# mLSTM heads run between the blocks of their own input projection, one core of a Trainium2 chip

## The chip, the cores and the metric

The kernel runs on one core of one Trainium2 chip. The metric is the device time of one execution in microseconds, before and after the change. Engines are named as in the profile: PE (TensorE), DVE (VectorE), ACT (ScalarE), POOL (GpSimd), SP (SyncE, which issues the weight transfers).

## What is computed

Two two-layer transformer blocks one after the other on 256 tokens of width 1024, in float32, with a squared-ReLU MLP after every mixer. The change touches the last mixer alone, an mLSTM:

```python
proj = h @ w_in                       # 1024 columns q,k; 1024 v; 1024 output gate; 8 gate columns
qk = silu(causal_depthwise_conv(qk, conv_w, conv_b))      # width 4
log_f = log_sigmoid(gates_f + b_f); i_pre = gates_i + b_i
ht = mlstm_chunkwise(q, k, v, i_pre, log_f)               # 4 heads, q and k 128 wide, v 256
out = sigmoid(o_pre) * rmsnorm(ht, head_norm_w)
return out @ w_out
```

## The kernel before

Activations lie transposed: 128 features on the partitions, 256 tokens along the free dimension. A weight matrix of 1024 rows is read as *blocks* of 128 columns, two per transfer (`load`, 1 MB). Each block is split into two float32r parts: ACT writes the high part (`split_hi`, line 465) and DVE the low part (`split_lo`, line 869). The parts lie in a ring of four (`RING`), so block b + 4 is split once PE has used block b (semaphore `w_used`). For one block of the input projection `linear` has PE do 8 x 3 matmuls of 256 columns (`product`, lines 1515 to 1517) into one of PSUM banks 0 to 3, which DVE reads out (line 843 writes `mz`) with the norm's factor `rstd`. The output projections use 8 pairs of matmuls per block (`paired`, lines 1521 and 1522).

All orders are written out by hand: each engine has its own program, runs it in order, and waits on semaphores. In the input projection a loop over j, here called a *slot*, runs on each engine. In slot j PE does block j; DVE reads block j and splits block j + 4; ACT splits block j + 4. The other work of the mixer hangs on slots:

- Blocks 0 to 7 are q and k, 8 to 15 the output gate, 16 the two gate rows (`M_GATE`), 17 to 24 v.
- `CONV_AT` says after which slot a q or k block gets its convolution: even ones on DVE (lines 1306 and 846), odd ones on POOL (lines 1486 to 1494). Then SiLU: ACT runs three functions (`log_sum`, lines 752 to 756), DVE a subtraction, ACT an exponential (line 769), POOL a product (line 1498).
- The output gate goes through `log_sum`, a subtraction on DVE and an exponential on ACT (`gate_exp`, line 760).
- The gate rows: DVE reads them and adds the biases in slot 16, ACT runs two functions in slot 17 (lines 782 and 784), DVE does two scans and some row operations in slot 18 (up to line 1329, semaphore `mg_rows`), and PE transposes the result after slot 22.

After all 25 blocks the four heads run in a loop of their own. PE transposes v to tokens (`m_value_tiles`, line 1908). Per head, `m_scores` spreads two gate rows over the partitions (line 1935) and forms the scores (line 1941). DVE adds and caps the arguments (`m_args`, line 1349), ACT takes exponentials, POOL masks, DVE multiplies (`m_products`). `m_sums` forms the denominators (line 1952) and the outputs (line 1957). Then ACT and DVE alternate: absolute value (line 802), logarithm, maximum, exponential, product `m_h` and square. PE sums the squares (line 1971), ACT takes two functions, DVE scales by the norm and the output gate, ACT copies the high part of `y`, DVE subtracts for the low part (line 1378, `y_ready`). Each role has two PSUM banks, so heads overlap in pairs.

The output projection (`out_proj`) then has on DVE, per block: a reduction of the two halves of the bank (line 882), the addition to the residual `h`, the low part of a later weight block, and the low part of the normed input `x` for the next MLP (`low_part`, line 846). The first block of that MLP takes the eight pieces of `x` in order.

## Time and profile before

| | us |
|---|---|
| median of three timed runs | 1318.15 |
| lowest, highest | 1315.78, 1324.64 |
| the profiled execution | 1322.65 |
| its span, first to last instruction | 1320.7 |

The span counts from the first to the last instruction and is 1.95 us shorter than the execution's time. Times in rows are from the span's start. The mLSTM mixer lies between about 985 and 1128 us.

### The profile page before, as it was taken

How to read it: one execution, taken by the hardware profiler on the slowest of the kernel's cores; microseconds unless marked ns; L12 is line 12 of the kernel's file. 1: busy time of each engine (PE TensorE's matmuls, PEld its weight loads, DVE VectorE, ACT ScalarE, POOL GpSimd, SP SyncE). 2: the span in 40 equal slices, each digit the busy share in tenths (PEclk: the TensorE clock that was granted, in tenths of full speed). 3: DMA queues.
4: the chain of work that ended last, by engine and by line, in shares of the span. 5: the costliest groups of instructions: out<-in, count | busy, mean ns of one | idle time of the engine just before them, and what ended most of it. 6: DMA issues, size and time to landing. Idle time of an engine off the chain costs nothing.

```text
span 1320.7 us, 24258 instructions
## 1 busy us (share of the span) xinstructions
PE 1253.3 (95%) x8344; PEld 1136.4 (86%) x8344; DVE 914.6 (69%) x1553; ACT 708.5 (54%) x1257; POOL 259.2 (20%) x277
## 2 busy tenths in 40 slices
PE   7999989999999999999999889999999888999996
PEld 6998889999999888888899668888889866888885
DVE  5778865555557987865666778786558857878563
ACT  4656645654444556654454665664445745666441
POOL 4000012210001034410000003441016511344010
PEclk9999999999999999999999889999999997999998
DMA  7414235655556556555555215555554432665540
GB/s 220 139 41 148 65 96 160 191 177 176 189 159 193 190 161 190 191 191 189 192 185 180 85 33 183 185 188 182 188 181 138 160 96 64 191 187 187 183 143 32
DMA packets 202389, 205.69 MB, mean 156 GB/s; under 512 B 6080, under 2 KB 199734, under 8 KB 202314
## 3 DMA queue, kind: packets, MB, share of 16 engines
q1 hardware_dynamic: 200053, 203.12, 48.1%
q10 hardware_dynamic: 2260, 1.58, 0.4%
q8 instruction: 45, 0.74, 0.2%
q14 instruction: 31, 0.25, 0.1%
HBM read 203.61 MB, written 1.06 MB: 155 GB/s over the span
## 4 chain that ended last, share of the span: by engine, by line
PE 77%; DVE 13%; ACT 5%; issue 3%; POOL 1%; DMA 0%; DVEq 0%; SPq 0%; POOLq 0%; ACTq 0%
PE PS L1521 28%; PE PS L1522 14%; PE PS L1515 10%; PE PS L1516 9%; PE PS L1517 9%; DVE wlo L869 4%; DVE x L846 2%; ACT whi L465 1%; DVE tmp L882 1%; DVE h L892 1%; PE PS L1671 1%; PE PS L1736 1%; PE PS L1714 1%; POOL mt L1491 1%; POOL mqk L1494 1%
## 5 line engine op out<-in xcount | busy, mean ns | idle before, releaser
L869 DVE TENSOR_TENSOR wlo<-raw,whi 128x1024 fp32r<-128x1024 f32 (+1 forms) x388 | 470.5, 1214 | 217.1 <-ACT whi L465 215.3
L465 ACT ACTIVATE whi<-raw 128x1024 fp32r<-128x1024 f32 (+1 forms) x388 | 404.6, 1046 | 333.3 <-PE PS L1522 215.9
L1521 PE MATMUL PS<-x,whi 128*128 128x512 f32 x832 | 293.7, 397 | 4.8 <-DVE x L846 4.5
L1515 PE MATMUL PS<-x,whi 128*128 128x256 f32 (+2 forms) x928 | 269.8, 291 | 10.8 <-DVE x L846 5.8
L1516 PE MATMUL PS<-x,whi 128*128 128x256 f32 (+2 forms) x928 | 267.5, 288 | 0.0
L1521 PE MATMUL PS<-hid,whi 128*128 128x512 f32 x768 | 267.0, 394 | 0.0
L1517 PE MATMUL PS<-x,wlo 128*128 128x256 f32 (+2 forms) x928 | 265.2, 286 | 0.0
L1522 PE MATMUL PS<-x,wlo 128*128 128x256 f32 x832 | 235.1, 283 | 0.0
L1522 PE MATMUL PS<-hid,wlo 128*128 128x256 f32 x768 | 212.7, 277 | 0.0
L1422 POOL TENSOR_TENSOR acc<-acc,sq 128x256 f32<-128x256 f32 (+2 forms) x72 | 63.9, 888 | 717.8 <-ACT sq L493 716.7
L1521 PEld LDWEIGHTS PS<-x,whi 128*128 128x128 f32 x832 | 157.0, 189 | 42.4 <-DVE x L846 6.4
L1515 PEld LDWEIGHTS PS<-x,whi 128*128 128x128 f32 x928 | 178.7, 193 | 13.8 <-DVE x L846 7.5
L1442 POOL TENSOR_TENSOR act_s<-act_r 128x256 f32<-128x256 f32 (+1 forms) x128 | 137.6, 1075 | 226.4 <-ACT act_r L510 152.9
L1517 PEld LDWEIGHTS PS<-x,wlo 128*128 128x128 f32 x928 | 177.7, 191 | 0.0
L1516 PEld LDWEIGHTS PS<-x,whi 128*128 128x128 f32 x928 | 177.2, 191 | 0.4
L1521 PEld LDWEIGHTS PS<-hid,whi 128*128 128x128 f32 x768 | 144.0, 188 | 33.4
L1522 PEld LDWEIGHTS PS<-x,wlo 128*128 128x128 f32 x832 | 158.0, 190 | 0.0
L882 DVE TENSOR_REDUCE tmp<-PS 128x256 f32<-128x512 f32 x152 | 104.8, 689 | 61.9 <-PE PS L1522 60.3
L1522 PEld LDWEIGHTS PS<-hid,wlo 128*128 128x128 f32 x768 | 144.2, 188 | 0.1
L1521 PE MATMUL PS<-y,whi 128*128 128x512 f32 x192 | 72.1, 416 | 2.1 <-DVE y L1378 1.8
L1516 PE MATMUL PS<-hid,whi 128*128 128x258 f32 x256 | 72.6, 284 | 0.0
L1515 PE MATMUL PS<-hid,whi 128*128 128x258 f32 x256 | 72.4, 283 | 0.0
(286 smaller groups left out, 1616.7 us busy)
## 6 DMA issues: line engine op xcount, KB each, us to landing
raw<-in_mlp_w SPq DMA_DIRECT2D x64, 1024.0 KB, 5.3
raw<-in_w_mlp_up SPq DMA_DIRECT2D x32, 1024.0 KB, 5.5
raw<-in_w_mlp_down SPq DMA_DIRECT2D x32, 1024.0 KB, 4.9
raw<-in_w_in_conv SPq DMA_DIRECT2D x12, 1024.0 KB, 5.1
raw<-in_attn_w_in SPq DMA_DIRECT2D x12, 1024.0 KB, 5.2
raw<-in_mlstm_w_in SPq DMA_DIRECT2D x12, 1024.0 KB, 5.2
raw<-in_w_in_attn SPq DMA_DIRECT2D x9, 1024.0 KB, 5.7
raw<-in_w_out_attn SPq DMA_DIRECT2D x4, 1024.0 KB, 5.4
```

Source lines behind the costliest of these rows:

```text
L465: A(part_view(whi, b), raw_view(b), ACT.Copy).then_inc(w_hi, 1)
L846: return V.scalar_tensor_tensor(out=o, in0=a, scalar=s, in1=b, op0=op0, op1=op1)
L869: V.tensor_tensor(part_view(wlo, b), raw_view(b), f32(part_view(whi, b)), ALU.subtract).then_inc(w_lo, 1)
L882: return V.tensor_reduce(o, PS[:, bk, :].rearrange("p (a t) -> p t a", a=2), mybir.AxisListType.X, ALU.add)
L892: V.tensor_tensor(at(h, j, tok), tmp[:, j % 2, 0:S], at(h, j, tok), ALU.add).then_inc(Z["out_h"], 1)
L1422: Gp.tensor_tensor(acc[:, 0:count], acc[:, 0:count], sq[:, k % 2, 0:count], ALU.add).then_inc(Z["acc_ready"], 1)
L1442: Gp.tensor_tensor(act_s[:, j % 2, 0:count], act_r[:, j % 2, 0:count], act_r[:, j % 2, 0:count], ALU.mult)\
L1515: mm(dst, whi_b, xs_hi, start=first, stop=False)
L1516: mm(dst, whi_b, xs_lo, start=False, stop=False)
L1517: return mm(dst, wlo_b, xs_hi, start=False, stop=last)
L1521: mm(dst.rearrange("p (a t) -> p a t", a=2), std_cols(whi[b % RING], k), xs_both, start=first, stop=False)
L1522: return mm(dst[:, S:2 * S], std_cols(wlo[b % RING], k), xs_hi, start=False, stop=last)
```

## The change

The blocks of the input projection come in another order (`M_Z` gives for each slot the part of `mz` that it fills; the gate block is in slot 4): q and k of head 0 and k and q of head 1 first, then v and output gate of head 0, then what the next head needs. The loads follow the same order. Each head's steps stand in the slots behind its last input: `S_AT` is the slot of its scores, `V_AT` of its value tiles; arguments one slot later, products and sums two, denominators and squares' input three, squares four, norm and gate five, the low part of `y` six. The loop has four slots more (`M_TAIL`), in which PE does the first six of eight pieces of output blocks 0 to 3, beside the last head. The last two pieces of these four blocks follow, and then blocks 4 to 7 whole. The heads use one PSUM bank per role instead of two: 7 for value tiles and outputs, 6 for scores, 5 for gate rows, 4 (`MISC`) for sums. Convolutions 3, 5 and 7 of the new order (`QK_POOL`) are on POOL, the other five on DVE; before it was four and four. PE waits for `mg_rows` after slot 7 (`M_GATE + 3`). The arithmetic is the same. The diff, cut:

```diff
-    add("m_in", "std", 2 * KB, 2)
+    add("m_in", "std", 4, 2)
     add("m_gate", "gate", 1, 1)
-    add("m_v", "std", KB, 2)
+    add("m_rest", "std", 20, 2)
...
-        M_GATE = 2 * KB
         M_BLOCKS = 3 * KB + 1
-        CONV_AT = {1 + 5 * f // 2: f for f in range(KB)}
-        LOG_AT = KB + 3
+        M_TAIL = 4
+        M_GATE = 4
+        M_Z = (0, 1, 4, 5, None, 16, 17, 8, 9, 2, 3, 18, 19, 10, 11, 6, 7, 20, 21, 12, 13, 22, 23, 14, 15)
+        QK_AT = (0, 2, 3, 1, 9, 10, 15, 16)
+        QK_POOL = (3, 5, 7)
+        QK_LOG = (2, 4, 5, 6, 10, 13, 16, 19)
+        O_AT = (7, 8, 13, 14, 19, 20, 23, 24)
+        V_AT = (7, 13, 19, 23)
+        S_AT = (7, 13, 19, 22)
...
-            thirds("m_in", wm, 2)
-            load(G["m_gate"], kpn(wm)[:, :, COL_GATES:COL_GATES + 2 * ML_HEADS], width=2 * ML_HEADS)
-            linear("m_v", wm, range(D, 2 * D, 2 * P))
+            for n, z in enumerate(M_Z[0:M_GATE:2] + M_Z[M_GATE + 1::2]):
+                if n == 2:
+                    load(G["m_gate"], kpn(wm)[:, :, COL_GATES:COL_GATES + 2 * ML_HEADS], width=2 * ML_HEADS)
+                c = z * P + (0 if z < KB else D if z < 2 * KB else -D)
+                load(G["m_in"] + n if n < 2 else G["m_rest"] + n - 2, kpn(wm)[:, :, c:c + 2 * P])
...
+            for j in range(M_BLOCKS + M_TAIL):
+                if j - 1 in V_AT:
+                    hd = V_AT.index(j - 1)
...
+                if j - 1 in S_AT:
+                    hd = S_AT.index(j - 1)
+                    act.wait_ge(Z["m_bc"], hd + 1)
+                    for t in range(TS):
...
+                if j - 3 in S_AT:
+                    hd = S_AT.index(j - 3)
...
+                if j - 5 in S_AT:
+                    hd = S_AT.index(j - 5)
...
+                if j - 6 in S_AT:
+                    hd = S_AT.index(j - 6)
...
+                if j == M_GATE + 1:
+                    act.wait_ge(Z["mg_abs"], 1)
+                    A(mgate[:, 2, :], mgate[:, 2, :], ACT.Exp, scale=-1.0).then_inc(Z["mg_ln"], 1)
+                    act.wait_ge(Z["mg_ln"], 1)
+                    A(mgate[:, 2, :], mgate[:, 2, :], ACT.Ln, bias=1.0).then_inc(Z["mg_ln"], 1)
...
+                if j in QK_LOG:
+                    c = QK_LOG.index(j)
+                    f = M_Z[QK_AT[c]]
+                    if c in QK_POOL:
+                        act.wait_ge(Z["mq_conv_odd"], QK_POOL.index(c) + 1)
+                    else:
+                        act.wait_ge(Z["mq_conv"], c + 1 - (c > 3) - (c > 5))
+                    if c >= 2:
+                        act.wait_ge(Z["mq_arg"], c - 1)
+                    log_sum(act_s[:, c % 2, 0:S], zb(mqk, f), Z["mq_log"], 3 * c)
...
+                if j - 2 in QK_LOG:
+                    c = QK_LOG.index(j - 2)
+                    f = M_Z[QK_AT[c]]
...
+                if j - 2 in O_AT:
+                    gate_exp(O_AT.index(j - 2))
+                if j < M_BLOCKS:
+                    split_hi(B["m_in"] + j + RING)
+                if j in O_AT:
+                    f = O_AT.index(j)
+                    act.wait_ge(psum_read, O["m_in"] + j + 1)
+                    if f >= 2:
+                        act.wait_ge(Z["ms_arg"], f - 1)
+                    log_sum(act_r[:, f % 2, 0:S], zb(og, f), Z["ms_log"], 3 * f)
...
-            for j in range(M_BLOCKS):
...
+            for j in range(M_BLOCKS + M_TAIL):
+                if j == M_GATE + 4:
+                    dve.wait_ge(Z["mg_t"], 1)
...
+                if j - 1 in S_AT:
+                    m_args(S_AT.index(j - 1))
+                if j - 2 in S_AT:
+                    m_products(S_AT.index(j - 2))
+                if j - 3 in S_AT:
...
+                if j - 5 in S_AT:
+                    hd = S_AT.index(j - 5)
...
+                    dve.wait_ge(Z["ms_done"], 2 * hd + 2)
...
+                if j - 6 in S_AT:
+                    hd = S_AT.index(j - 6)
...
+                if j - 1 in QK_LOG:
+                    c = QK_LOG.index(j - 1)
+                    f = M_Z[QK_AT[c]]
...
+                if j - 1 in O_AT:
+                    f = O_AT.index(j - 1)
...
                 if j == M_GATE + 2:
                     dve.wait_ge(Z["mg_ln"], 2)
...
+                if j >= M_BLOCKS:
+                    continue
+                dve.wait_ge(w_used, B["m_in"] + j + 1)
+                if j == M_GATE:
+                    gp = PS[:, bank("m_in", j), 0:S]
...
+                split_lo(B["m_in"] + j + RING)
+                if j == M_GATE:
...
+                if j in QK_AT and QK_AT.index(j) not in QK_POOL:
+                    f = M_Z[j]
+                    acc_f, z_f = zb(mqk, f), zb(mz, f)
+                    dve.wait_ge(psum_read, O["m_in"] + j + 1)
...
-                    for f in range(KB + 1):
-                        if f % 2:
-                            acc_f, z_f = mqk[:, f * S:(f + 1) * S], mz[:, f * S:(f + 1) * S]
-                            pool.wait_ge(psum_read, O["m_in"] + f + 1)
+                    for c in range(KB):
+                        if c in (0, 4, 6):
+                            u = (0, 4, 6).index(c)
+                            j = QK_AT[QK_POOL[u]]
+                            f = M_Z[j]
+                            acc_f, z_f = zb(mqk, f), zb(mz, f)
+                            pool.wait_ge(psum_read, O["m_in"] + j + 1)
...
-                        if f >= 1:
-                            pool.wait_ge(Z["mq_exp"], f)
-                            Gp.tensor_tensor(zb(mqk, f - 1), zb(mqk, f - 1), zb(mt1, f - 1), ALU.mult).then_inc(Z["mq_done"], 1)
...
+                        f = M_Z[QK_AT[c]]
+                        pool.wait_ge(Z["mq_exp"], c + 1)
+                        Gp.tensor_tensor(zb(mqk, f), zb(mqk, f), zb(mt1, f), ALU.mult).then_inc(Z["mq_done"], 1)
+                        if c in (2, 4, 6, 7):
+                            hd = (2, 4, 6, 7).index(c)
+                            for t in range(TS):
+                                pool.wait_ge(Z["m_w"], TS * hd + t + 1)
+                                tri = m_e[:, hd % 2, t, t * P:(t + 1) * P]
+                                Gp.affine_select(out=tri, in_=tri, compare_op=ALU.is_ge, fill=0.0, base=0, pattern=[[1, P]],
+                                                 channel_multiplier=-1).then_inc(Z["m_mask"], 1)
...
+            def m_value_tiles(hd):
+
+                last_v = (6, 12, 18, 22)[hd]
+                pe.wait_ge(psum_read, O["m_in"] + last_v + 1)
+                if hd:
+                    pe.wait_ge(Z["m_hn"], hd)
                 for a in range(TS):
-                    for f in range(KB // 2):
-                        c = (2 * KB + half * (KB // 2) + f) * S + a * P
-                        last = nc.tensor.transpose(PS[:, bank0 + a, f * P:(f + 1) * P], mz[:, c:c + P], ident[:, :])
+                    for f in range(2):
...
             def m_scores(hd):
-                r = hd % 2
-                if hd >= 2:
-                    pe.wait_ge(Z["m_arg"], TS * (hd - 1))
...
+                if hd == 0:
+                    pe.wait_ge(Z["sel_in"], 16)
+                else:
+                    pe.wait_ge(Z["m_arg"], TS * hd)
+                    pe.wait_ge(Z["m_em"], hd)
 
                 for half, row in ((0, 9), (1, 7)):
-                    last = mm(PS[:, r, half * S:(half + 1) * S], sel[:, hd * P:(hd + 1) * P], mgate[:, row, :], start=True, stop=True)
+                    last = mm(PS[:, 5, half * S:(half + 1) * S], sel[:, hd * P:(hd + 1) * P], mgate[:, row, :], start=True, stop=True)
...
-                    pe.wait_ge(Z["m_pr"], TS * (hd - 1))
+                pe.wait_ge(Z["mq_done"], (2, 4, 7, 8)[hd])
+                if hd:
+                    pe.wait_ge(Z["m_pr"], TS * hd)
...
+                    mm(PS[:, 6, j * S + j * P:(j + 1) * S], mqk[:, (4 + hd) * S + j * P:(4 + hd) * S + (j + 1) * P],
...
             def m_sums(hd):
...
+                    last = mm(PS[:, MISC, j * P:S], ones[:, :], m_p[:, r, j, j * P:S], start=(j == 0), stop=(j == TS - 1))
                 last.then_inc(Z["m_nd"], 1)
+                pe.wait_ge(Z["m_vtok"], hd + 1)
...
+            def m_out(j, ks):
+
+                b = B["m_out"] + j
+                if ks[0] == 0:
+                    free_bank("m_out", j)
+                    pe.wait_ge(w_lo, b + 1)
+                for k in ks:
+                    pe.wait_ge(Z["y_ready"], 24 + k // 2 + 1)
+                    last = paired(b, k, at(yh, k, LAST), both(yh, k, LAST), PS[:, bank("m_out", j), :], k == 0, k == KB - 1)
+                if ks[-1] == KB - 1:
+                    last.then_inc(w_used, 1)
+
+            for j in range(M_BLOCKS + M_TAIL):
+                if j < M_BLOCKS:
+                    linear("m_in", j, xh, xl, LAST, x_blocks(6) if j == 0 else None)
+                else:
+                    m_out(j - M_BLOCKS, range(6))
+                if j == 1:
+                    norm(6, S)
+                if j == M_GATE + 3:
+                    pe.wait_ge(Z["mg_rows"], 1)
+                    pe.wait_ge(Z["norm_read"], 7)
+                    for a in range(TS):
+                        last = nc.tensor.transpose(PS[:, MISC, a * ML_HEADS:(a + 1) * ML_HEADS], mgate[:, 5, a * P:(a + 1) * P],
+                                                   ident[0:ML_HEADS, 0:ML_HEADS])
+                    last.then_inc(Z["mg_t"], 1)
+                if j - 4 in S_AT:
+                    m_squares(S_AT.index(j - 4))
+                if j - 2 in S_AT:
+                    m_sums(S_AT.index(j - 2))
+                if j in V_AT:
+                    m_value_tiles(V_AT.index(j))
+                if j in S_AT:
+                    m_scores(S_AT.index(j))
+            for j in range(4):
+                m_out(j, range(6, KB))
+            for j in range(4, KB):
+                m_out(j, range(KB))
```

## Rows read from the trace of the kernel before

**Rows 1.** The page, part 1: busy us, share of span, instructions.
```profile
PE 1253.3 (95%) x8344; PEld 1136.4 (86%) x8344; DVE 914.6 (69%) x1553; ACT 708.5 (54%) x1257; POOL 259.2 (20%) x277
```

**Rows 2.** Windows: stretch, length, busy (count) PE, PEld, DVE, ACT, POOL; clock, DMA share, GB/s.
```profile
985.00:1062.00 77.00, 72.56 (x591) 71.83 (x591) 60.72 (x98) 48.79 (x93) 41.81 (x37) 0.98 0.50 154
1000.00:1020.00 20.00, 20.00 (x171) 20.00 (x170) 14.60 (x22) 11.41 (x19) 13.26 (x13) 1.00 0.50 142
1062.00:1102.00 40.00, 26.95 (x118) 20.32 (x118) 19.80 (x42) 19.48 (x43) 2.41 (x9) 0.87 0.15 48
1102.00:1128.00 26.00, 24.49 (x131) 21.02 (x130) 23.16 (x31) 14.15 (x24) 6.06 (x8) 0.93 0.40 122
```

**Rows 3.** Timeline of DVE, start of the projection: start, duration, instruction.
```profile
991.46 0.42 DVE L843 TENSOR_TENSOR mz<-PS,rstd 128x256 f32<-128x256 f32 x1
...
994.40 0.41 DVE L1306 TENSOR_SCALAR mqk<-mz,vec_b 128x256 f32<-128x256 f32 x1
...
996.40 0.42 DVE L843 TENSOR_TENSOR mz<-PS,rstd 128x256 f32<-128x256 f32 x1
```

**Rows 4.** Timeline of ACT: first log function, then the next weight splits.
```profile
996.51 0.42 ACT L752 ACTIVATE act_s<-mqk 128x256 f32<-128x256 f32 x1 [3.76 <-DVE mqk L846]
...
997.73 1.99 ACT L465 ACTIVATE whi<-raw 128x1024 fp32r<-128x1024 f32 x2
```

**Rows 5.** Timeline of DVE around the gate rows.
```profile
1036.74 0.84 DVE L843 TENSOR_TENSOR mgate<-PS,rstd 4x256 f32<-4x256 f32 x2
...
1038.75 0.83 DVE L1306 TENSOR_SCALAR mqk<-mz,vec_b 128x256 f32<-128x256 f32 x1
...
1041.34 0.82 DVE L1317 TENSOR_SCALAR mgate<-mgate,vec_b 4x256 f32<-4x256 f32 x1
...
1042.89 0.40 DVE L846 SCALAR_TENSOR_TENSOR mz<-mz,act_r 128x256 f32<-128x256 f32 x1
...
1047.83 0.41 DVE L846 SCALAR_TENSOR_TENSOR mgate<-mgate 4x256 f32<-4x256 f32 x1
...
1051.37 0.41 DVE L846 SCALAR_TENSOR_TENSOR mt<-mqk,act_s 128x256 f32<-128x256 f32 x1
```

**Rows 6.** Timeline of all engines, the heads.
```profile
1062.57 1.09 PE L1908 MATMUL PS<-ident,mz 128*128 128x128 f32 x8 [0.52 <-DVE mz L843]
...
1063.59 1.13 PE L1935 MATMUL PS<-mgate,sel 4*128 4x256 f32 x4
...
1065.50 1.12 PE L1935 MATMUL PS<-mgate,sel 4*128 4x256 f32 x4
...
1068.08 0.89 PE L1952 MATMUL PS<-m_p,ones 128*128 128x256 f32 x4 [0.61 <-DVE m_p L846]
...
1070.21 1.13 PE L1935 MATMUL PS<-mgate,sel 4*128 4x256 f32 x4
...
1072.42 0.36 ACT L802 ACTIVATE m_d<-PS 128x256 f32<-128x256 f32 x1
...
1075.67 1.13 PE L1971 MATMUL PS<-m_sq,ones 128*128 128x256 f32 x4 [0.68 <-ACT m_sq L814]
...
1094.37 2.07 PE L1971 MATMUL PS<-m_sq,ones 128*128 128x256 f32 x4 [4.95 <-ACT m_sq L814]
...
1098.64 0.87 DVE L846 SCALAR_TENSOR_TENSOR m_h<-m_h,vec_b,m_rs 128x256 f32<-128x256 f32 x2
...
1101.01 0.69 DVE L1378 TENSOR_TENSOR y<-m_h,y 128x512 fp32r<-128x512 f32 x1 [0.77 <-ACT y L823]
```

**Rows 7.** Timeline of DVE in the output projection: first, second and last reduction.
```profile
1102.76 0.69 DVE L882 TENSOR_REDUCE tmp<-PS 128x256 f32<-128x512 f32 x1 [1.06 <-PE PS L1522]
...
1107.10 0.69 DVE L882 TENSOR_REDUCE tmp<-PS 128x256 f32<-128x512 f32 x1 [1.09 <-PE PS L1522]
...
1125.66 0.68 DVE L882 TENSOR_REDUCE tmp<-PS 128x256 f32<-128x512 f32 x1
```

**Rows 8.** Window of POOL during one of its convolutions.
```profile
1008.71:1016.97 8.26, 7.72 (x9) 1.00 0.43 127
```

More of the change, by code:

```diff
@@ L785, in _ @@
[L785 to L799 removed]
+                A(zb(og, f), zb(og, f), ACT.Exp).then_inc(Z["ms_done"], 1)
@@ L808, in _ @@
-                if 0 <= hd < ML_HEADS:
                     act.wait_ge(Z["m_dmax"], hd + 1)
@@ new lines, in _ @@
+                if j in QK_AT and QK_AT.index(j) not in QK_POOL:
+                    f = M_Z[j]
+                    acc_f, z_f = zb(mqk, f), zb(mz, f)
+                    dve.wait_ge(psum_read, O["m_in"] + j + 1)
+                    step(V.tensor_scalar(acc_f, z_f, vb("mlstm_conv_w_2", 3 * KB + f), vb("mlstm_conv_b_2", f), ALU.mult, ALU.add))
+                    for back in (1, 2, 3):
+                        ins = stt(acc_f[:, back:], z_f[:, 0:S - back], vb("mlstm_conv_w_2", (3 - back) * KB + f), acc_f[:, back:],
+                                  ALU.mult, ALU.add)
+                        if back < 3:
+                            step(ins)
+                        else:
+                            ins.then_inc(Z["mq_conv"], 1)
@@ L1973, in _, with m_squares @@
-            out_proj("m_out", 3, LAST)
+            def m_squares(hd):
+                pe.wait_ge(Z["m_hsq"], hd + 1)
+                pe.wait_ge(Z["m_abs"], 2 * hd + 1)
+                for a in range(2):
+                    last = mm(PS[:, MISC, S:2 * S], ones[:, :], m_sq[:, a, :], start=(a == 0), stop=(a == 1))
+                last.then_inc(Z["m_ss"], 1)
+            def m_out(j, ks):
[8 more added lines that the diff above has]
+                    last.then_inc(w_used, 1)
```

257 lines of the change are left out of this document (75 added, 182 removed).

## The prediction

> **What bounds the kernel now.** I read the page's busy line first: PE has work in 95% of the span, DVE in 69%, ACT in 54% [rows 1]. So only a stretch in which PE waits can give time back. The windows show where that is [rows 2]. From 985 to 1062 us the mLSTM input projection runs with PE busy 72.56 of 77.00 us. From 1062 to 1102 us the four heads run alone: PE is busy 26.95 of 40.00 us, DVE 19.80, ACT 19.48, and the granted clock is 0.87. These 40 us are a ladder of small steps from engine to engine, and they are what the change goes after. From 1102 to 1128 us is the output projection, where DVE is busy 23.16 of 26.00 us. Its timeline [rows 7] shows one reduction every 3.09 us ((1125.66 - 1107.10)/6), while PE needs only some 2.8 us per block. DVE paces this stretch. The next stage's first matmul group needs the last piece that this DVE chain writes, so the chain's start sets everything after it. In the trace that start is 1102.76 us, 1.06 us after the last head's low part is written at 1101.01 + 0.69 = 1101.70 [rows 6, 7]. I call that last write T. The question is how far T moves.
>
> The profiled execution took 1322.65 us around a span of 1320.7; the three timed runs have a median of 1318.15. I work out a difference in the profiled one and put it on the median.
>
> **Part 1, heads moved between the blocks.** Nothing is computed less: the same 25 blocks, the same head matmuls, the same weight loads in another order (13 transfers before and after, hidden as before: the DMA share is 0.50 in this stretch [rows 2], and each still waits only for a ring slot). What could go is PE's waiting. A block costs PE 24 matmuls at 20.00/171 = 0.117 us [rows 2], 2.81 us; some records can be missing, so up to 2.85. A head costs PE 0.51 us of value transposes (half of 1062.57 to 1063.59), 1.91 for gate rows and scores (1063.59 to 1065.50), 2.13 for sums and outputs (1068.08 to 1070.21), and 1.13 for the squares [rows 6]. If PE never waited, the heads would add about 22 us to the projection and T would come some 9 us earlier.
>
> **Part 2, the gates come too early for DVE.** This decides the sum. The gate block is now the fifth (slot 4), and PE asks for the finished gate rows right after slot 7, before any head. In slots 0, 2 and 3 DVE has a convolution each, and it can read no block before 991.46 us, when the norm is ready [rows 3]. Walk DVE's queue. Slot 0: read and the small split of the gate block, 0.5, convolution 2.0 (994.40 to 996.40): 994.0. Slot 1: read and full split 1.47 (the trace has two of them between 991.46 and 994.40): 995.4. Slot 2: ACT now runs the first log chain (1.22) and then the split's high part (1.0) from 994.0 on [rows 4], so DVE's low part starts at 996.3 and ends by 997.6; the convolution beside POOL takes 2.59 (1038.75 to 1041.34 [rows 5]): 1000.2. Slot 3: subtraction 0.4, read and split 1.6, convolution 2.6: 1004.8. Slot 4: gate read 0.87, split 1.2, gate adds 1.55 (1041.34 to 1042.89) [rows 5]: 1008.4. Then ACT, in this order: two gate functions of at most 0.42 each, the log chain 1.22, the high part 1.0 [rows 4]: 1011.5. DVE, still in slot 5, waits for that high part, and needs 1.2 for the split, 0.4 for a subtraction, 3.54 for the gate rows (1047.83 to 1051.37) [rows 5]: 1016.6. PE will have ended block 7 near 1005.9 (block 0 is finished at 985, seven more at 2.85, and the norm's matmul between). So PE waits about 10.7 us in one piece, and its head work cannot start. With every convolution at 2.0 and no split stretched the rows come at 1014.9; with every one at 2.6 and a split stretched by POOL, at 1018. Even in the trace of before the path from gate read to rows takes 14.6 us (1036.74 to 1051.37) [rows 5], but there PE has six blocks to do between the gate block and the rows' use, here three.
>
> **Part 3, from there to the last head.** PE from 1016.6: gate transposes 0.4, values 0.5, rows and scores 1.9: 1019.4. Then seventeen blocks at 2.83, 48.1; four times sums, 8.5; three more value tiles, 1.5, and rows with scores, 5.7; three squares, 3.3: 67.1 us, so 1086.5. Two additions. After so long a wait the clock: in the trace the four matmuls of the squares take 1.13 us after a wait of 0.68 and 2.07 after one of 4.95 [rows 6], and a clock of 0.87 over 40 us [rows 2] is about 10 us at the lower of the two levels; I take one such spell, 2 us lost, bounds 0 and 4. And small waits in slots 13, 15, 19 and 21, where DVE's products or POOL's third convolution end with PE already there: 1.5 us, bounds 0 and 4 (POOL: a convolution is 8.26 us [rows 8], and its end in slot 19 and PE's need coincide). DVE itself has room: 60.72 + 19.80 us of work [rows 2] and 2.6 for the fifth convolution over some 105 us. In sum the last head's sums end at 1090.0; in the trace they end at 1086.1.
>
> The Trainium skill ("TensorE: Matmul & The Clock Gate", Part 1) says that the array is slowed by default and that activity releases it. The squares' two durations agree. By that rule without the row the sum would be the same 2 us.
>
> **Part 4, the tail beside the output projection.** With one bank per role, and with each engine taking its steps in slot order, the last head's ladder is no shorter. ACT finishes the last output gate's logs first, about 0.7 us past the sums. Absolute value to squares is 3.25 (1072.42 to 1075.67) [rows 6]. PE's first output block stands at its fifth piece until head 2's low part is written, 1.46 later (an idle 0.77 for ACT's copy and DVE's subtraction of 0.69, the row at 1101.01 [rows 6]). Then PE does 0.7 of that block, 2.1 of the next, and only then the squares, 1.13; two ACT functions 0.9; scale, gate, copy and subtraction 3.06 (1098.64 to 1101.70) [rows 6]. That is 13.3 us: T = 1103.3, against 1101.70.
>
> **Part 5, after T.** The four blocks begun early need two pieces each, so the chain starts at T + 1.06 = 1104.4, and its second step is no longer late: in the trace the first step is 4.34 us (1102.76 to 1107.10), because PE ran at the lower level, the others 3.09 [rows 7]. This gives 1.3 back: the last reduction is at 1104.4 + 7 x 3.09 = 1126.0, against 1125.66. But the four blocks done early leave PE with only four in 25 us, then with one piece of the next stage per 3.09 us. Its clock will fall there, where in the trace it does not, and the next stage is bound by PE: I add 2 us, bounds 0 and 3. Together 0.3 + 2 = 2.3, rounded to 2.5 since the ladder's terms leave no gap between engines.
>
> **Part 6, the fifth convolution on DVE.** It costs DVE 2.6 and frees POOL of 8.26 us. It is priced above. The Trainium skill ("GPSIMD Engine Reference", Key points) says that POOL shares its SBUF interfaces with DVE for DVE instructions with two SBUF inputs; the rows' 2.00 and 2.59 for one convolution are both beside POOL, so neither is shown as free of it. By the rule one POOL convolution less gives DVE up to 1 us back, off PE's path after slot 7.
>
> **Forecast:** 1318.15 + 2.5 = 1320.6 us, no change that can be told: about 1% is what a measurement of this kernel can tell from none. Chance 0.55; its own range 1315 to 1325.
>
> **Rivals.**
> (A) The gate wait is short, because DVE and ACT catch up. For it: PE waits a microsecond less for each that DVE saves before slot 7, and DVE idles in the trace. Against: the shortest sum of rows is still 9 us of wait. Without the wait T is 1093 and the time 1318.15 - 8.7 - 1.3 + 2 = 1310. Chance 0.2, mostly of something in between, 1311 to 1315.
> (B) Slower: the low clock. Place: PE after each wait, from slot 7 to the next stage's start. Price: half of the time spent at the lower level. It decides once the low level holds for more than 8 us between 1017 and 1090: then four more spells cost 8 us and the time is 1328.6; if it holds for 25 us, 1333. For it: 0.87 in the trace's head stage. Against: 1.00 in stretches with work in every slot [rows 2]. Chance 0.17.
> (C) The change does not do what it says: the heads' steps stand in slots, but the ping-pong of ACT and DVE within a slot (largest value, exponential, product) delays the splits, and DVE paces the stage at some 4 us a slot. 17 slots at 4.1 from 1019.4 are 1089.1, the last sums 2.1 more, 1.2 later than forecast: 1322. Chance 0.08.
>
> **How the numbers follow.** The low end takes A's 1310 as the rare case and leaves little below 1312; the high end takes B's 1328.6: range 1312 to 1328. Faster by over 1% means below 1305, which even no wait at all does not reach: 0.04 is left for a term that I have missed. Slower by over 1% is above 1331.3, the far half of B: 0.06. Within: 0.90.
>
> **What would show it.** In the profile of the changed kernel: one PE wait of 9 to 12 us near 1006, released by DVE's gate rows or the copy of the value block; no other PE wait over 3 us until the output projection; last head's sums near 1090; DVE's reductions 3.09 apart from the first; a clock below 1.00 at the start of the next stage; POOL's waits harmless. I am wrong if PE's wait for the gates is under 5 us, if DVE is busy over 90% from 1020 to 1090, or if the last reduction of the output projection starts over 5 us away from 1126.

## The result and the profile after

Twenty runs of each kernel: 1318.29 us before, 1324.39 us after (1322.18 to 1330.23). The ratio is 1.0046, interval 1.003 to 1.0062: the change costs 4 to 8 us, 0.5%. The forecast was 1320.6 in 1312 to 1328: no change over 1%, and a small loss. The profiled execution of after took 1326.36 us around a span of 1324.6. One execution of e9_conv_behind, a kernel of the experiments, took 3086.61 us and is left out of its ratio.

All times below are also given from one event, DVE's first read of a block of this projection: 991.46 us before [rows 3], 987.33 after. The code ahead of it is the same in both kernels, and in the profiled executions of this study it lay anywhere from 983.85 to 992.56 us, so absolute times of two traces can't be subtracted, but times from that read can. In the forecast they are the time less 991.46.

The page's busy line is as before [rows 1]:

```profile
PE 1253.3 (95%) x8344; PEld 1135.5 (86%) x8344; DVE 915.9 (69%) x1557; ACT 709.2 (54%) x1259; POOL 244.2 (18%) x270
```

Where PE waited between 985 and 1137 us (line, releaser, total us, times, longest):

```profile
PE PS L1992 <- DVE mgate L1381: 10.3, 1, 10.3
PE PS L1537 <- DVE x L860: 5.5, 3, 2.4
PE PS L1537 <- DVE y L1362: 4.2, 1, 4.2
PE PS L1923 <- DVE mz L857: 1.2, 2, 0.6
PE PS L1952 <- DVE m_p L860: 0.7, 3, 0.2
```

The ladder of the four heads [rows 2, 6] is gone as a stretch, and its waits have become one: 10.3 us for the gate rows. DVE's timeline up to it:

```profile
987.33 0.42 DVE L857 TENSOR_TENSOR mz<-PS,rstd 128x256 f32<-128x256 f32 x1
...
987.81 0.41 DVE L1401 TENSOR_SCALAR mqk<-mz,vec_b 128x256 f32<-128x256 f32 x1
988.25 1.52 DVE L860 SCALAR_TENSOR_TENSOR mqk<-mz,vec_b,mqk 128x255 f32<-128x255 f32 x3
...
993.25 0.83 DVE L1401 TENSOR_SCALAR mqk<-mz,vec_b 128x256 f32<-128x256 f32 x1
994.12 1.95 DVE L860 SCALAR_TENSOR_TENSOR mqk<-mz,vec_b,mqk 128x255 f32<-128x255 f32 x3
...
1000.34 0.84 DVE L857 TENSOR_TENSOR mgate<-PS,rstd 4x256 f32<-4x256 f32 x2
...
1006.47 1.23 DVE L883 TENSOR_TENSOR wlo<-raw,whi 128x1024 fp32r<-128x1024 f32 x1 [2.28 <-ACT whi L473]
...
1011.70 0.27 DVE L1381 TENSOR_SCALAR mgate<-mgate 4x256 f32<-4x256 f32 x1
```

Gate read at 1000.34, 13.0 us from the first read; then the 2.28 us in which DVE waits for a high part that stands on ACT behind the two gate functions and a log chain; last row written at 1011.97, 24.64 us. The windows (length, busy and count of PE, PEld, DVE, ACT, POOL; granted clock; DMA share; GB/s):

```profile
987.33:1012.03 24.70, 14.41 (x123) 14.20 (x121) 21.17 (x40) 12.23 (x23) 10.01 (x10) 0.84 0.41 128
1012.00:1021.00 9.00, 8.97 (x34) 7.57 (x35) 4.38 (x9) 2.93 (x8) 1.27 (x3) 0.50 0.36 117
1042.00:1046.00 4.00, 4.00 (x21) 3.82 (x21) 2.57 (x6) 2.95 (x8) 0.74 (x2) 0.59 0.83 262
1060.00:1090.00 30.00, 29.18 (x215) 27.05 (x214) 22.50 (x39) 20.30 (x42) 5.82 (x10) 1.00 0.45 140
1092.00:1100.00 8.00, 4.82 (x15) 4.15 (x16) 1.76 (x4) 2.29 (x5) 0.00 (x0) 0.57 0.42 130
1128.00:1132.00 4.00, 2.89 (x8) 2.09 (x9) 2.62 (x5) 2.60 (x4) 0.73 (x1) 0.50 0.25 83
```

In the first row DVE is busy 21.17 of 24.70 us, and 2.28 us of the rest is its wait for ACT: that is why the rows are late. In the second PE is busy throughout, at a clock of 0.50, the lower of the two levels (1.2 GHz): 34 matmuls in 9 us, where the fourth row has 215 in 30. The third, fifth and sixth are three more such spells (a *spell* is here a stretch at the lower level). The fourth is what the change was to give: PE busy 97% of the time, with head work between the blocks.

The tail, from PE's and DVE's timelines:

```profile
1095.18 0.79 PE L1537 MATMUL PS<-y,whi 128*128 128x512 f32 x1 [4.22 <-DVE y L1362]
...
1100.20 1.02 PE L1966 MATMUL PS<-m_sq,ones 128*128 128x256 f32 x4
```

```profile
1104.53 0.69 DVE L1362 TENSOR_TENSOR y<-m_h,y 128x512 fp32r<-128x512 f32 x1 [0.70 <-ACT y L807]
1106.28 0.69 DVE L896 TENSOR_REDUCE tmp<-PS 128x256 f32<-128x512 f32 x1 [1.05 <-PE PS L1538]
1109.46 0.68 DVE L896 TENSOR_REDUCE tmp<-PS 128x256 f32<-128x512 f32 x1
...
1127.87 0.68 DVE L896 TENSOR_REDUCE tmp<-PS 128x256 f32<-128x512 f32 x1
```

These answer to [rows 6, 7]. Between the wait for `y` and the squares PE does eight pairs of output matmuls in 5.02 us, nearly all at the low level. T, the end of the last low part of `y`, is 1104.53 + 0.69 = 1105.22, the eighth reduction 1127.87.

### The profile page after: what moved, and what is told of

It is laid out like the page before. It is cut to its first block, busy times and chain, and to the rows that moved or that the text cites. A ratio compares the mean times of both kernels' runs of the same rounds, so it can differ in the third digit from the quotient of the medians.

```text
span 1324.6 us, 24248 instructions
## 1 busy us (share of the span) xinstructions
PE 1253.3 (95%) x8344; PEld 1135.5 (86%) x8344; DVE 915.9 (69%) x1557; ACT 709.2 (54%) x1259; POOL 244.2 (18%) x270
## 4 chain that ended last, share of the span: by engine, by line
PE 78%; DVE 14%; ACT 4%; issue 3%; DMA 0%; DVEq 0%; SPq 0%; POOLq 0%; ACTq 0%; POOL 0%
PE PS L1537 28%; PE PS L1538 14%; PE PS L1531 10%; PE PS L1532 10%; PE PS L1533 10%; DVE wlo L883 4%; DVE x L860 2%; ACT whi L473 2%; DVE tmp L896 1%; DVE h L906 1%; PE PS L1687 1%; PE PS L1752 1%; PE PS L1730 1%; DVE mqk L860 1%; ACT x L497 0%
```

## The experiments

Twelve kernels, each timed in 5 rounds (11 or 12 runs) beside the kernel before on the same chip. "8th" is the start of the eighth reduction of DVE and "12th" that of the twelfth, the fourth of the next stage, both in us from DVE's first read, in the one profiled execution. The ratio is against the kernel before (medians 1317.6 to 1318.9 us in the four groups of runs).

| kernel | median us | ratio (interval) | gate wait | 8th | 12th |
|---|---|---|---|---|---|
| before | 1318.29 | 1 | none | 134.20 | 145.61 |
| after | 1324.39 | 1.0046 (1.003, 1.0062) | 10.3 | 140.54 | 153.67 |
| e1_fill | 1322.54 | 1.0039 (1.002, 1.0058) | 0.8 | 136.79 | 150.08 |
| e2_rows_early | 1322.86 | 1.0032 (1.0013, 1.0051) | 6.3 | 135.83 | 148.99 |
| e3_tail_order | 1322.24 | 1.0023 (1.0006, 1.004) | 10.3 | 133.21 | 146.01 |
| e4_no_tail | 1319.44 | 0.9996 (0.9978, 1.0015) | 10.3 | 133.51 | 146.46 |
| e5_late2 | 1323.08 | 1.0034 (1.0013, 1.0055) | 1.1 | 139.36 | 152.46 |
| e6_all_tail | 1315.95 | 0.9974 (0.9954, 0.9994) | 2.4 | 130.48 | 144.56 |
| e7_all_no_tail | 1317.52 | 0.9986 (0.9966, 1.0007) | 2.4 | 130.95 | 142.34 |
| e8_tail_warm | 1319.18 | 1.0001 (0.9983, 1.0019) | 10.3 | 133.76 | 146.70 |
| e9_conv_behind | 1325.87 | 1.0058 (1.0038, 1.0078) | 8.5 | 139.25 | 152.51 |
| e10_conv_all | 1319.35 | 0.9999 (0.9979, 1.002) | 4.4 | 132.13 | 145.46 |
| e11_conv_late | 1316.88 | 0.9985 (0.9965, 1.0005) | 1.5 | 130.47 | 143.52 |
| e12_conv_apart | 1316.13 | 0.9981 (0.9962, 1.0) | 1.5 | 129.01 | 142.73 |

An interval is some 5 us wide, so steps of 2 us between kernels are read from the traces. The two agree: the 12th reduction's distance from the kernel before (8.1 us for after, -2.9 for e12_conv_apart) is within 2.7 us of the ratio's (6.1 and -2.5) in every line.

One thing in the traces is no effect of an edit. The spell of the third window above (1041.8 to 1045.2 us) is in the profiled execution of after alone: e1_fill, e2_rows_early, e3_tail_order, e4_no_tail and e8_tail_warm have the same orders there and run it at full clock. Between the same two blocks, those of slots 13 and 14, DVE's reads are 5.4 us apart in after and 3.8 to 3.9 in these five. So 1.6 us of each difference from after in the columns "8th" and "12th" belong to that execution, for these five at least.

**e1_fill: is it the wait, or the low clock that it leaves?** Throwaway matmuls occupy PE while DVE works; they are extra work whose result nobody reads.

```diff
                 if j == M_GATE + 3:
+                    for _ in range(84):
+                        mm(PS[:, 6, 0:S], x2[:, 0:P], at(xh, 1, LAST), start=True, stop=True)
                     pe.wait_ge(Z["mg_rows"], 1)
```

> Changed kernel with 84 throwaway matmuls of PE put between block 7 and its wait for the gate rows (they write a bank that nothing reads; about 10 us of work). Clock theory (the 10.3 us wait itself is fixed by DVE, but the low clock behind it costs some 4 us more): the wait shrinks to under 1.5 us, the gate rows come at the same time, the granted clock from 1012 to 1021 us goes from 0.50 to 1.00, and the kernel is 3.5 to 4.5 us faster than the changed kernel (ratio to before about 1.001). Rival (the slow stretch after the wait is something else, or the fill only moves the spell): no gain, ratio 1.004 to 1.006.

The rows end where they did (24.68 us), and the clock stays at 1.00 while PE is occupied. But head 0's small matmuls follow, and a spell of some 3 us at the low level comes there:

```profile
1005.00:1011.00 6.00, 5.14 (x46) 4.86 (x45) 5.72 (x12) 3.53 (x7) 1.70 (x2) 1.00 0.09 30
1013.00:1016.00 3.00, 3.00 (x15) 2.96 (x14) 1.86 (x5) 2.53 (x8) 0.88 (x3) 0.50 0.97 283
```

The eighth reduction comes 3.75 us earlier than in after, but only part of that is the fill's. Block 8 is read 2.5 us earlier (32.06 us after the first read instead of 34.57); 1.6 us are the spell that only after's execution has, and the tail gives 0.3 back. So in the trace the fill is worth 2.5 us: the 4.3 us that the spell behind the wait cost, less what the new one takes. The times don't show it: the ratio of 1.0039 can't be told from after's 1.0046, and the 1.001 that was expected lies below its interval. The rival had it in part, since the fill also moves the spell. The wait itself stays, hidden under work for nothing.

**e2_rows_early: who is late?** DVE's ten row operations stand ahead of its low part in slot 5, since ACT's gate functions are done before that low part's high part.

```diff
                     mul(zb(mz, M_Z[j]), PS[:, bank("m_in", j), 0:S], rstd[:, 0:S]).then_inc(psum_read, 1)
+                if j == M_GATE + 1:
+                    dve.wait_ge(Z["mg_ln"], 2)
...
                 split_lo(B["m_in"] + j + RING)
```

> Changed kernel with DVE's gate rows put into slot 5, between its read of block 5 and its low part, instead of the start of slot 6. Theory (PE's wait is set by DVE's queue ahead of the rows: 2.3 us idle for ACT's high part, 1.2 us of split, 0.4 of subtraction): rows about 4 us earlier, PE's wait 10.3 to about 6.5 us, the clock still falls; 3.5 to 4.5 us faster than the changed kernel, ratio to before about 1.001 to 1.002. Rival (DVE and ACT pace the whole stage, so the time comes back in later slots): ratio 1.004 to 1.006, and new PE waits of some 4 us in slots 8 to 24.

Rows at 20.63 us instead of 24.64, PE's wait 6.3 us instead of 10.3: the order on DVE sets the rows, and the wait follows them microsecond for microsecond. The eighth reduction is 4.7 us earlier, 3.2 of it at block 8 (read at 31.36 us) and 1.6 the spell that is missing. The ratio, 1.0032, is above the 1.001 to 1.002 expected, and can't be told from after's.

**e3_tail_order and e4_no_tail: the tail.** e3 gives PE the output blocks in pieces: 0 to 3 of four blocks, the last head's squares, pieces 4 and 5, then 6 and 7. e4 has no output block beside the last head: the squares come first, and all blocks whole behind them.

```diff
-            for j in range(M_BLOCKS + M_TAIL):
-                if j < M_BLOCKS:
-                    linear("m_in", j, xh, xl, LAST, x_blocks(6) if j == 0 else None)
-                else:
-                    m_out(j - M_BLOCKS, range(6))
+            for j in range(M_BLOCKS):
+                linear("m_in", j, xh, xl, LAST, x_blocks(6) if j == 0 else None)
...
+            for j in range(4):
+                m_out(j, range(4))
+            m_squares(3)
+            for j in range(4):
+                m_out(j, range(4, 6))
```

> Changed kernel with PE's tail in another order: pieces 0 to 3 of output blocks 0 to 3, then the last head's squares, then pieces 4 and 5 of each, then 6 and 7. Theory (the tail is late because PE waits 4.2 us for head 2's low part with work at hand, runs then at the lower clock, and does the squares only behind two blocks): last low part 4.5 to 5.5 us earlier, the wait gone, ratio to before 1.000 to 1.001. Rival (the ladder of ACT and DVE sets the last head's end whatever PE does): under 1.5 us earlier, ratio 1.004 to 1.005.

> Changed kernel with one part undone: no output block runs beside the last head; the squares come right behind the sums, and all eight output blocks after the last low part. If the early blocks are worth what the forecast gave them (their chain starts 2.2 us earlier and its second step is 1.2 us shorter) but cost the squares 4 to 7 us of delay and the next stage a spell of low clock: this kernel is 1 to 4 us faster than the changed kernel, ratio to before 1.002 to 1.004. Rival (running part of the projection beside the last head is a net gain): slower than the changed kernel by 2 us or more, ratio 1.006 to 1.008.

In e3 the wait for `y` of head 2 is gone, and the window that had 4.82 us of PE work at 0.57 in after is full and at full clock (window; then PE's and DVE's timelines):

```profile
1092.00:1100.00 8.00, 8.00 (x46) 6.99 (x46) 3.65 (x7) 4.78 (x11) 0.00 (x0) 1.00 0.44 134
```

```profile
1089.51 0.81 PE L1952 MATMUL PS<-m_p,ones 128*128 128x256 f32 x4
...
1097.08 1.03 PE L1966 MATMUL PS<-m_sq,ones 128*128 128x256 f32 x4
```

The squares start 7.6 us after the last denominators (1097.08 - 1089.51), in after 12.8 (1100.20 - 1087.43). Of the 7.3 us by which the eighth reduction is earlier, 5.2 are this, as expected (4.5 to 5.5); the other 2.1 lie ahead of it, 1.6 of them the spell that only after's execution has. The ratio, 1.0023 (from 1.0006), came out above the 1.000 to 1.001 expected. e4 ends at the same place, since there PE waits 4.37 us for the squares' input and does them at the low level:

```profile
1088.83 1.53 PE L1966 MATMUL PS<-m_sq,ones 128*128 128x256 f32 x4 [4.37 <-ACT m_sq L795]
```

So the output blocks beside the last head, in the order of the change, are worth less than nothing: leaving them out is 7.0 us better in the trace, 5.4 of them without the spell of after's execution, and 5 in the median, and the two intervals don't meet. That is more than the 1 to 4 us expected. They are in the squares' way.

**e5_late2: give PE two more blocks before it asks for the rows.** Gate transposes, head 0's value tiles and scores stand behind slot 9, and what follows them in head 0 two slots later too.

```diff
-        V_AT = (7, 13, 19, 23)
-        S_AT = (7, 13, 19, 22)
+        V_AT = (9, 13, 19, 23)
+        S_AT = (9, 13, 19, 22)
...
-                if j == M_GATE + 3:
+                if j == M_GATE + 5:
```

> Changed kernel with the use of the gate rows and head 0's values and scores behind slot 9 instead of slot 7; the other heads stay. The mLSTM stage (DVE's first read of the projection to its last reduction in the output projection) is 134.2 us in the kernel before and 140.5 in the changed one. Gate theory: PE does blocks 8 and 9 in the time in which it waited; the one wait of 10.3 us becomes three short ones of some 4.5 us in sum (for low parts and then for the rows), the clock stays up, and the stage takes 131 to 134 us; ratio to before 0.998 to 1.000. Rival (DVE and ACT pace the stage; the wait only let them catch up): PE waits in later slots instead, stage over 137 us, ratio over 1.002.

The wait moved; this is the rival's case. PE waits 1.1 us for the rows, and then in slot 11 (PE's, and DVE's timeline):

```profile
1033.51 1.62 PE L1952 MATMUL PS<-m_p,ones 128*128 128x256 f32 x4 [7.68 <-DVE m_p L860]
```

```profile
1025.58 0.41 DVE L1401 TENSOR_SCALAR mqk<-mz,vec_b 128x256 f32<-128x256 f32 x1
...
1031.61 1.23 DVE L883 TENSOR_TENSOR wlo<-raw,whi 128x1024 fp32r<-128x1024 f32 x1 [2.88 <-ACT whi L473]
```

DVE comes to head 0's arguments late, behind a low part and the convolution of slot 9; ACT takes the exponentials and then a log chain before its next high part; DVE waits 2.88 us for that high part, with the products behind it. The gate wait was the place where DVE's backlog showed, not its cause.

**e6_all_tail and e7_all_no_tail: all at once.** Rows early, head 0 behind slot 8 (one slot later), and the tail of e3 or of e4.

```diff
-        V_AT = (7, 13, 19, 23)
-        S_AT = (7, 13, 19, 22)
+        V_AT = (8, 13, 19, 23)
+        S_AT = (8, 13, 19, 22)
```

> Rows early, head 0 one slot later (behind slot 8), and the tail in the order of the run with pieces 0 to 3 first. If the terms add: 134.2 - 1 (tail order left it at 133.2) less 7 us of wait and 4 of low clock: stage 122 to 125 us. The next stage still begins at the lower clock, since PE has run out of work before it: ratio to before 0.993 to 0.996. If DVE and ACT pace the stage, over 128 us and ratio over 0.997.

> As the run before it, but with no output block beside the last head: squares right behind the sums, then all eight blocks. Stage 122 to 126 us as well, and the next stage begins at full clock, which is worth 1.5 to 2 us more: ratio to before 0.991 to 0.995, the fastest of all. If beginning the output blocks early is what counts, it is 2 us slower than the run before it.

Both missed the reduction that was expected (122 to 126 us) and came 10 us ahead of after; at over 128 us it is the case in which DVE and ACT pace the stage. The expected lead of e7 over e6 did not come in the times either (1317.52 and 1315.95). e6_all_tail is the fastest median of all and its whole interval lies below the kernel before, by 0.8 to 6 us. Its waits are now many small ones: 2.4 us for the rows, 2.6 for products, 2.1 for the copy of a value block, 0.9 for a low part. The two differ in what follows. The 15 us from 125 to 140 us after the first read, around the eighth reduction, first e6, then e7:

```profile
1113.61:1128.61 15.00, 9.53 (x34) 7.32 (x33) 11.00 (x17) 7.37 (x13) 3.22 (x4) 0.66 0.47 148
```

```profile
1112.56:1127.56 15.00, 13.37 (x76) 11.22 (x75) 12.69 (x18) 8.46 (x15) 4.56 (x5) 1.00 0.50 157
```

With four blocks nearly done, PE has little to do while DVE's chain runs, and its clock falls to 0.66; from the 8th to the 12th reduction e6 takes 14.1 us, e7 11.4, as the kernel before does (145.61 - 134.20).

**e8_tail_warm: can that be bought back?** e3_tail_order with 40 throwaway matmuls ahead of the next MLP, extra work again.

```diff
             for j in range(4, KB):
                 m_out(j, range(KB))
+            for _ in range(40):
+                mm(PS[:, 6, 0:S], y2[:, N_META:N_META + P], at(yh, 1, LAST), start=True, stop=True)
```

> Tail order as in that run, with 40 throwaway matmuls of PE behind the last output block, before the next MLP (4.7 us of work in a bank that nothing reads). Clock theory for the next stage: in the tail-order run PE idles there and the next stage's first matmuls run at the lower clock; here they run at 1.00, and the time from the last reduction to the tenth is 1.5 to 2 us shorter, ratio 0.001 to 0.0015 below the tail-order run's 1.0023. Rival (the spell does not depend on PE's idleness there): no change.

From the 8th to the 12th reduction it takes 12.9 us, e3 12.8: nothing gained in the trace. The ratio is 0.0022 lower than e3's, inside both intervals. The clock holds at 1.00 until 1118 us and then falls to 0.83 (1118 to 1124), so this settles only that forty don't help there.

**e9_conv_behind: take a convolution out of DVE's way.** The block of slot 3 (k of head 1) is not needed before slot 13; its convolution runs in slot 7, behind the rows.

```diff
-        QK_AT = (0, 2, 3, 1, 9, 10, 15, 16)
-        QK_POOL = (3, 5, 7)
-        QK_LOG = (2, 4, 5, 6, 10, 13, 16, 19)
+        QK_AT = (0, 2, 1, 3, 9, 10, 15, 16)
+        QK_POOL = (2, 5, 7)
+        QK_LOG = (2, 4, 5, 8, 10, 13, 16, 19)
...
-                if j in QK_AT and QK_AT.index(j) not in QK_POOL:
-                    f = M_Z[j]
+                if j in (0, 2, 7, 9, 15):
+                    f = M_Z[3 if j == 7 else j]
```

> The changed kernel with one DVE convolution moved: the one of the block of slot 3 (k of head 1, not needed before slot 13) runs in slot 7, behind the gate rows, and its logarithms in slot 8. Theory (DVE's backlog sets the gate rows: DVE was busy 21.2 of the first 24.7 us): the rows end 2.6 us earlier, 22.0 us after DVE's first read instead of 24.6, PE's wait falls from 10.3 to 7.7 us, and since the moved convolution lies where DVE has room, the eighth reduction comes 2.6 us earlier, 137.9 instead of 140.5: 1321.8 us. Rival (ACT sets them: its two gate functions stand behind the log chains and the splits' high parts, so DVE only waits longer for ACT): the rows stay within 1 us of 24.6 and the time at 1324. Second rival (the backlog only moves, as in e5_late2): rows at 22, but PE then waits 2 to 3 us for head 0's products or a low part in slots 8 to 10, and the time stays at 1323 to 1324.

The rows end at 22.85 us, 1.8 earlier instead of 2.6, and PE's wait is 8.5. Then PE waits 2.8 us for the products of head 1, where after waits 0.2, and the eighth reduction gains 1.3 us in all. The second rival had the right kind of wait and size, though one head later than it said. In the times nothing is gained: 1325.87 us, and the 1321.8 expected (a ratio of 1.003) lies below the interval.

**e10_conv_all, e11_conv_late, e12_conv_apart: the same move in the good versions.** e10 has the rows early and e3's tail, e11 is e6_all_tail with it, e12 also moves the next convolution behind the products of head 0, and ACT's logarithms of the first moved one from slot 8 to slot 9.

```diff
-        QK_LOG = (2, 4, 5, 8, 10, 13, 16, 19)
+        QK_LOG = (2, 4, 5, 9, 12, 13, 16, 19)
...
-                if j in (0, 2, 7, 9, 15):
-                    f = M_Z[3 if j == 7 else j]
+                if j in (0, 2, 7, 11, 15):
+                    f = M_Z[{7: 3, 11: 9}.get(j, j)]
```

> The same move together with the gate rows ahead of DVE's low part in slot 5 (e2_rows_early) and the tail's order of e3_tail_order; head 0 stays behind slot 7. Theory: the three savings add up. Rows at 20.6 - 2.6 = 18 us after DVE's first read, PE's wait 3.7 us, no low clock behind it; the eighth reduction at 133.2 - 6.6 + some 2 that e3 had already got from the clock = 128.6, against 130.5 of e6_all_tail: 1314.5 us. Rival (below a wait of some 6 us PE is held by the next thing, DVE's products and ACT's high parts, as e6_all_tail and e5_late2 showed): PE's waits between 14 and 60 us after the first read still sum to 6 us or more, the eighth reduction is at 130.5 or later, and the time is 1316 or more.

> e6_all_tail (gate rows early, head 0 behind slot 8, tail order) with the convolution of slot 3 moved to slot 7. Theory: e6_all_tail's remaining waits in the head (2.4 us for the gate rows, 2.6 for head 0's products, 2.1 for a read block) come from DVE's backlog of the early convolutions, so taking 2.6 us from it takes about as much from them: gate wait under 0.5, products under 1.5, the eighth reduction at 127.5 to 128.5 instead of 130.5, 1313.5 us, ahead of both kernels. Rival (the waits for products are the length of the ladder of head 0, arguments, exponentials, mask, products, between two slots, and not a backlog): the gate wait goes and the products' wait grows by as much, eighth reduction at 130 or later, 1316.

> e11_conv_late with two more steps moved: DVE's convolution of slot 9's block (q of head 2) runs in slot 11, behind the products of head 0, with its logarithms in slot 12; and ACT takes the logarithms of the convolution in slot 7 in slot 9 instead of 8. In e11_conv_late DVE did a 1.9 us convolution directly ahead of the products for which PE had been waiting 3.6 us, and stood still 1.7 and 1.0 us for ACT's high parts, since ACT itself waited 1.9 us for a convolution ahead of one of them. Theory (these two orders hold the products): the wait for products falls from 3.6 to under 1 us, and the eighth reduction comes at 127.5 to 128.5 instead of 130.5 us after DVE's first read: 1314.5 us, ratio about 0.997. Rival (the ladder of head 0 itself, value block read, arguments, exponentials, mask, products over slots 9 and 10, is that long whatever else DVE does, or the wait comes back at the next step): PE's waits between 14 and 60 us stay at 7 us or more in sum and the eighth reduction stays within 1 us of 130.5.

e10 fell to its rival: 132.13, not 128.6. So did e11: its wait for the rows is down from 2.4 to 1.5 us and the one for head 0's products up from 2.1 to 3.6, and the eighth reduction stays where e6_all_tail has it (130.47). DVE's timeline shows what stands ahead of those products:

```profile
1018.26 0.41 DVE L1401 TENSOR_SCALAR mqk<-mz,vec_b 128x256 f32<-128x256 f32 x1
1018.70 1.52 DVE L860 SCALAR_TENSOR_TENSOR mqk<-mz,vec_b,mqk 128x255 f32<-128x255 f32 x3
1020.14 0.61 DVE L860 SCALAR_TENSOR_TENSOR m_p<-PS,m_e 128x256 f32<-128x256 f32 x2
```

e12 takes that convolution away (and moves ACT's logarithms with it, so the two steps aren't told apart), and PE's rows say what it brought:

```profile
1020.54 0.89 PE L1952 MATMUL PS<-m_p,ones 128*128 128x256 f32 x4 [1.13 <-DVE m_p L860]
1043.78 0.89 PE L1952 MATMUL PS<-m_p,ones 128*128 128x256 f32 x4 [3.62 <-DVE m_p L860]
```

Head 0's wait falls from 3.6 to 1.1, and head 1 now has one of 3.6: PE's waits between 14 and 60 us still sum to 7.7, as the rival said. The eighth reduction is 1.5 us earlier (129.01), half of what was expected; the median, 1316.13, can't be told from e6_all_tail's 1315.95. Whether the two convolutions could be placed so that neither head waits was not tried. Nor was the gate block in a slot later than 4, the fifth convolution back on POOL, or two PSUM banks per role: what these three parts of the change cost or give is not shown apart.

## Why the prediction was right, and where its sum was off

The sign and the class were right, and the time in the range, but the forecast of +2.5 us lies under the measured interval, +4 to +8. By the prediction's own steps, in us from DVE's first read:

- **Part 2 (the gate rows)** held. Rows at 24.64 against 1016.6 - 991.46 = 25.1; one wait of 10.3 us against 10.7, released by the rows. Undone in parts by e2, e9 and e11, it shrank to 6.3, 8.5 and 1.5 us.
- **Part 3 (from the rows to the last sums)** was the first mis-sized term. It allowed 73.4 us (1090.0 - 1016.6); it took 77.6 (1089.56, the end of the last outputs, less 1011.97). The small waits were 1.9 us (1.2 and 0.7) against 1.5. The rest is the clock: one spell at 2 us was allowed, a price taken from rows of the heads, where PE's waits were 5 us and less [rows 6], and the spell behind 10.3 us was longer. The one behind the gate wait held from 1012 to 1021.3, and block 8 was read at 1021.90, 9.9 us after PE went on; at the full clock these matmuls are 0.4 + 0.5 + 1.9 + 2.8 = 5.6 us by the prediction's rows, so it cost 4.3. A second spell, of 3.4 us, behind a pause of 0.6 us at head 1's value tiles, cost 1.6; five other executions with the same orders did without it, so it was bad luck of this execution more than a price of the kernel. e1_fill, which puts a shorter spell in the place of the first, gains 2.5 at that block.
- **Part 4 (the tail)** was the second: 15.7 us from the last sums to T (1105.22 - 1089.56) against 13.3. The order of steps was as forecast. The wait for head 2's low part was 4.2 us, and behind it the 2.8 us of output matmuls that stand before the squares took 5.0 at the low level. The prediction had the wait and did not carry the clock through it. In the kernel before the same distance is 15.6 us (1101.70 - 1086.1), so the new tail gave nothing; with the order of e3_tail_order it is 10.5 (T at 110.57, the last outputs' end at 100.1, both from the first read).
- **Part 5 (after T)** held: reductions every 3.08 us ((1127.87 - 1106.28)/7), and a clock of 0.50 at the next stage's start. From the 8th to the 12th reduction 13.1 us against 11.4 before: 1.7 us, forecast 2.
- **Part 6 (the fifth convolution)** held for the slots ahead of the gate rows: the two convolutions beside POOL's took 2.82 and 2.64 us. Over the whole kernel it was priced too high. DVE's busy time grew by 1.3 us (914.6 to 915.9) and not 2.6, since three of its five convolutions (slots 0, 9 and 15) now run beside none of POOL's and take 1.96 us each; POOL's fell by 15.0 us (259.2 to 244.2) and not 8.26.

Of the rivals, A (a short wait) fell by the 10.3 us. B (low clock) was the one to lean to. By absolute time the low level held 7.7 us between 1017 and 1090, just under the 8 named; counted from the first read the same stretch is 1012.9 to 1085.9 in this trace, and there it held 11.8 us, so B's condition was met. Its time, 1328.6, was not reached, because B's sum adds 8 us for four more spells where its own price, half of the time at the lower level, gives 5.9 us for 11.8, or 3.9 over the 2 allowed. The clock took 3.9 us more than allowed there and 2.2 in the tail. That is what the forecast lacked: its eighth reduction was at 134.5 (1126.0 - 991.46), the trace's is at 140.5. C (DVE paces the stage) fell: 22.50 of 30 us busy, with PE at 29.18. Of the signs named, the gate wait, the reductions' distance and the clock at the next stage's start came; "no other PE wait over 3 us until the output projection" too; the last reduction, within 2 us of 1126 by the absolute time, is 6 us late by the time from the first read, which is over the 5 allowed: that is the mis-sized clock.

In the traces after stands 8.06 us behind before at the 12th reduction; the medians say 6.1. The difference of 2 us is the size of what one execution's spells move; 1.6 of it is the one that the other five executions lack.

The Trainium skill ("TensorE: Matmul & The Clock Gate", Part 1) calls the slow clock the default, which activity releases; the trace agrees in that the clock was 0.50 when PE went on after the gate wait and rose to 1.00 while it worked, but only after 9.3 us of continuous matmuls. What follows for a forecast is the lesson of Part 3: the wait is paid, and then the work behind it is paid at half speed.

## What to carry to other kernels

When independent work is interleaved to fill an engine's idle time, look at the first place where it needs a result from the engine that is catching up: the idle time gathers there. Moving the consumer later only moves the wait to the next product of the late engine; what helped was to put the short step that others wait for ahead of the long ones (the gate rows before a low part, the squares before output blocks). Price a PE wait of several microseconds as the wait plus the low clock after it (here 10.3 + 4.3, and 4.2 + 2.2). And before a difference between two traces is put down to an edit, see in which blocks it arises: 1.6 of the 3.75 us that e1_fill seemed to gain were a spell of one execution elsewhere.

## What was not expected

- **A pause of 0.6 us followed by a spell.** PE was idle for 0.6 us at 1039.4, between two stretches of full work; at 1041.8 the clock fell to the lower level and stayed there for 3.4 us in which PE was busy all the time. In e3_tail_order the same instructions, behind a pause of 0.60, ran at 1.00, and so did they in the four other kernels with these orders. What decides between the two is not shown. A stretch at 100% busy is no proof of the full clock.
- **A convolution costs DVE up to 0.9 us more beside POOL's, and how much depends on what POOL does.** In slot 0, before POOL starts, it took 1.96 us (987.81 to 989.77); in slot 2, beside POOL's, 2.82 (993.25 to 996.07, the stretched pair of rows above), in slot 3 2.64. But the kernel before has one beside POOL's that took only 2.00 [rows 3]. The first operation tells them apart. It reads one 256-column input and two vectors. Beside POOL's operation with two inputs (`TENSOR_TENSOR`) it takes 0.83 us at 993.25 in after; beside POOL's operation with one (`TENSOR_SCALAR`) it took 0.41 at 994.40 in before, as it does alone. POOL's row in before, then in after:

```profile
993.47 1.61 POOL L1486 TENSOR_SCALAR mqk<-mz,vec_b 128x256 f32<-128x256 f32 x1 [8.09 <-DVE mz L843]
```

```profile
992.78 1.15 POOL L1509 TENSOR_TENSOR mqk<-mqk,mt 128x255 f32<-128x255 f32 x1
```

  In the 14 profiled executions this operation takes 0.72 to 0.84 us in this mixer where it meets POOL's `TENSOR_TENSOR` and 0.40 or 0.41 elsewhere; beside `TENSOR_SCALAR` alone there is this one case. The three operations behind it take 1.52 us alone and 1.95 in slot 2. The Trainium skill ("GPSIMD Engine Reference", Key points) says that POOL shares its SBUF interfaces with DVE for instructions with two SBUF inputs, and the trace agrees for these three; the doubling of the first shows that an instruction with one tensor input can be held up too.
